# Where an expert's tokens sit in its half tile: consecutive rows, or rows 0, 8, 16, ... in turn

## The chip, the cores and the metric

One Trainium2 chip, one of its NeuronCores. The metric is the time of one execution on the device, in microseconds; the median of three executions of the kernel before is 883.63 us (880.76 to 884.49).

## What is computed

A float32 decoder trunk of two layers over 512 tokens of width 1024. Each layer is a mixer (gated spatial mixing and sparse attention in layer 0, a causal pooling in layer 1) and then a mixture of experts. Only the experts matter here:

```python
lg = xn @ w_rg + b_rg;  g_sel = argmax(lg)            # one of 4 groups
le_sel = (xn @ w_re + b_re)[group g_sel]              # 8 experts of the group
top_v, top_i = top_k(le_sel, 2)                       # the two best
h = silu(xn @ w_gate[e]) * (xn @ w_up[e])             # 1024 -> 256, each chosen expert
y += weight * (h @ w_down[e])                         # 256 -> 1024
```

There are 32 experts a layer, each with 3 MB of weights, and each token goes to two of them: 1024 token slots a layer. The slots that each expert gets come out of the router. Computed with the reference on its own inputs they are, two experts (a pair) at a time from pair 0 to pair 15:

```
layer 0: 29,39  17,25  41,30  51,34  24,39  45,29  35,27  54,47  28,21  16,43  19,43  29,29  30,17  27,25  32,42  31,26
layer 1: 18,22  25,16  19,16  21,15  21,26  49,39  37,36  49,45  42,51  23,49  32,41  46,30  19,21  21,40  42,41  43,29
```

## The kernel before, in words

**The pair loop.** The experts of a layer are worked off in 16 pairs. A pair has a tile of 128 rows: 64 for its first expert, 64 for its second. `slot0` (line 634) gives each expert its base, and a token's slot is that base plus the token's rank within the expert, so the 39 tokens of an expert have ranks 0 to 38. What would overflow 64 goes to extra pairs; with the counts above there is none, and the code for them (lines 678 to 692) runs no iteration.

**The tables.** `route` (DVE, lines 1361 to 1473) turns the routing into two tables of row numbers with one-hot matrices. Line 1438 is where the row of the tile is fixed: `OA[p, a, n]` is 1 where `col128[n]` equals the token's slot number within the pair (`pm`). Before, `col128[n] = n` (line 630). TensorE multiplies `OA` by the pair one-hots (line 1884), and the result, indexed by row n and pair, becomes `gather_at` (line 1446) and `scatter_at` (line 1444). A row without a token gets the number 4096 for the scatter and 3584 for the gather, which the bounds check leaves out. The last pair is not scattered: its rows are added by a matmul with `pair_mix`, which is made of the same `OA` (lines 1466 to 1473). So everything that uses the row order takes it from `OA`.

**The transfers of a pair.** POOL issues a gather of a pair's token rows from `norm_dram` into `xg` (line 653, 128 row numbers, 4 KB a row, one SBUF partition a row) and, after the pair is computed, a scatter of its result rows from `ys` into `out_dram` (line 659). That makes 16 gathers and 15 scatters a layer. The gather of pair i + 2 is issued once TensorE has transposed pair i. SP issues the weights in the order of use into three buffers (lines 535 to 568): four transfers of 1 MB for gate and up, two of 1 MB for down; the last pair's down comes in halves. A weight transfer writes the same bytes to each of the 128 partitions. SP waits for TensorE to have finished pair i - 3 before it loads pair i.

**Engines.** TensorE transposes the gathered rows (line 1892), does gate and up (line 1898, 32 recorded matmuls a pair), transposes the hidden rows (line 1905) and does down (line 1912, 16). It waits for a pair's weights by semaphore. After the last pair come the sums over the two experts of a token (lines 1110, 1114, 2000), for which SP reads `out_dram` back (line 572).

**Data movement.** All transfers run on the core's 16 DMA engines. A transfer counts as landed when every engine that had a part of it is through with that part.

Of the kernel before, what the change touches and what calls it, by code (L numbers as in the profile page):

```python
# [24 lines left out]
P = 128  # L25
# [11 lines left out]
TILE = 64  # L37
# [8 lines left out]
def build(nc, t):  # L46
    ctx = ExitStack()
    with ctx:
        def sb(name, cols, dt=F32, parts=P):
            return ctx.enter_context(nc.sbuf_tensor(name, [parts, cols], dt))  # L50
# [18 lines left out]
        col128 = sb("col128", P)  # L69
# [333 lines left out]
        def _(sp):  # L403
# [15 lines left out]
            def load_win(ch):  # L419
                _, c0, n = CH[ch]  # L420
                dst = win[ch % 2][:, 0:KD * n].rearrange("p (k n) -> p k n", k=KD)
                src = t["w_in"][0].rearrange("(p k) n -> p k n", k=KD)[:, :, c0:c0 + n]
                sp.dma_start(dst, src).then_inc(s_w[ch], 16)
# [168 lines left out]
        def _(pool):  # L592
            g = nc.gpsimd
            count = [0]

            def link(ins):

                count[0] += 1
                ins.then_inc(s_gp, 1)
                pool.wait_ge(s_gp, count[0])  # L600
# [26 lines left out]
            select(c3[0], NEG, -31, [[P, NB], [-16, 32]], 1)  # L627
            select(c3[1], 0.0, -31, [[P, NB], [-16, 32]], 1)
            io = dict(allow_small_or_imprecise_dtypes=True)
            link(g.iota(col128[:, :], [[1, P]], base=0, channel_multiplier=0, **io))  # L630
            link(g.iota(col32[:, :], [[1, 32]], base=0, channel_multiplier=0, **io))
            link(g.iota(tok_lo[:, :], [[0, 1]], base=0, channel_multiplier=1, **io))
            link(g.iota(tok_hi[:, :], [[1, 2 * NB]], base=-int(EMPTY) // P, channel_multiplier=0, **io))
# [1445 lines left out]
```

## Time and profile before

| | |
|---|---|
| median of 3 executions | 883.63 us |
| the profiled execution | 885.34 us, its span 883.6 us |
| TensorE busy | 790.1 us, mean granted clock 0.967 |
| DVE, ACT, POOL busy | 249.8, 244.6, 99.6 us |
| mean DMA rate over the span | 292 GB/s |
| packets of the POOL queue (gathers, scatters) | 16.27 MB in 8928 packets |
| packets of the SP queue | 241.16 MB in 67056 packets |

The profile has two expert stages. In layer 0 the loads of pair 3 are issued at 335 us and the last pair's gate and up finish at 556 us; in layer 1 these are 635 and 861 us. In both the DMA engines move some 420 GB/s, and outside of them much less. "Granted clock" is the share of full speed at which TensorE was allowed to run. "issue" in a chain is time in which an engine waited for nothing that the profile records. The profiled execution was 1.7 us slower than the median.

### The profile page before, as it was taken

What the parts mean: (1) busy time and instruction counts of PE and PEld (TensorE: products, weight loads), DVE (VectorE), ACT (ScalarE), POOL (GpSimd) and SP (SyncE); (2) the same over time, 40 slices, a digit from 0 to 9 for tenths busy, and PEclk for the clock granted to TensorE, in tenths of its full rate; (3) what the DMA queues carried; (4) which work ended last, traced back from release to release, by engine and by line L of the source; (5) the groups of instructions that cost most, each with busy time, mean ns of one, the idle gap of its engine ahead of it and who ended that gap; (6) DMA issues with size and microseconds to landing.
All of it is one profiled execution on the core that took longest, in us unless ns stands there. A gap on an engine that the chain in (4) does not pass through costs nothing.

```text
span 883.6 us, 10297 instructions
## 1 busy us (share of the span) xinstructions
PE 790.1 (89%) x3966; PEld 376.2 (43%) x3973; DVE 249.8 (28%) x565; ACT 244.6 (28%) x587; POOL 99.6 (11%) x167
## 2 busy tenths in 40 slices
PE   7999999999999989999787987898999987797975
PEld 6544544454555633333332332496433332232321
DVE  1012428566452351111011111545411110111106
ACT  4321436644344401211111111454121221111101
POOL 2000000000003510111001010040111111101000
PEclk9999999999999999999998999999999998898998
DMA  7996130300003987999999999997399999999975
GB/s 257 237 330 256 55 96 1 96 1 1 1 1 99 342 352 297 418 420 419 421 422 419 418 409 376 387 421 318 136 400 420 419 420 421 422 419 416 413 302 228
DMA packets 76032, 258.09 MB, mean 292 GB/s; under 512 B 28113, under 2 KB 29649, under 8 KB 56016
## 3 DMA queue, kind: packets, MB, share of 16 engines
q1 hardware_dynamic: 67056, 241.16, 69.8%
q0 software_dynamic: 8928, 16.27, 4.9%
q8 instruction: 32, 0.52, 0.2%
q14 instruction: 16, 0.13, 0.0%
HBM read 247.44 MB, written 26.21 MB: 310 GB/s over the span
## 4 chain that ended last, share of the span: by engine, by line
PE 75%; DMA 8%; DVE 6%; issue 4%; ACT 3%; SPq 3%; DVEq 0%; POOLq 0%; ACTq 0%
PE ps L1898 23%; PE ps L1624 11%; PE ps L1912 11%; PE ps L1776 6%; PE ps L1892 4%; DMA w_pair<-in_w_exp_up_dram 3%; PE ps L1689 3%; DMA rest<-in_w_exp_down_dram 2%; PE ps L1832 2%; SPq L443 2%; PE ps L1701 2%; PE ps L1844 2%; PE ps L2027 2%; PE ps L1606 2%; PE ps L1589 2%
## 5 line engine op out<-in xcount | busy, mean ns | idle before, releaser
L1898 PE MATMUL ps<-w_pair,tmp 128*64 128x512 f32 x704 | 170.9, 640 | 34.8 <-issue 21.3
L1898 PEld LDWEIGHTS ps<-w_pair,tmp 128*64 128x64 f32 x704 | 55.8, 147 | 136.1 <-issue 122.5
L1624 PE MATMUL ps<-w_pair,norm 128*128 128x512 f32 (+1 forms) x256 | 100.5, 553 | 1.4 <-ACT norm L803 1.4
L1088 DVE TENSOR_TENSOR tmp<-tmp,ps 128x256 f32<-128x256 f32 (+1 forms) x34 | 13.8, 407 | 294.8 <-ACT tmp L973 294.7
L973 ACT ACTIVATE tmp<-ps 128x256 f32<-128x256 f32 x32 | 12.3, 383 | 271.4 <-PE ps L1898 271.4
L1898 PE MATMUL ps<-norm,tmp 128*64 128x512 f32 x320 | 74.8, 621 | 12.2 <-issue 9.2
L1912 PE MATMUL ps<-w_pair,tmp 128*64 128x512 f32 x352 | 80.4, 598 | 3.1 <-ACT tmp L976 2.0
L1624 PEld LDWEIGHTS ps<-w_pair,norm 128*128 128x128 f32 x256 | 49.4, 195 | 49.3 <-issue 44.6
L659 POOL DMA_INDIRECT expert_rows<-tmp x30 | 30.1, 1003 | 327.0 <-DVE tmp L1491 327.0
L1776 PE MATMUL ps<-w_pair,norm 128*128 128x512 f32 x128 | 58.0, 593 | 0.0
L968 ACT ACTIVATE tmp<-ps,gains 128x128 f32<-128x128 f32 x128 | 36.5, 368 | 62.3 <-PE ps L1892 62.3
L1898 PEld LDWEIGHTS ps<-norm,tmp 128*64 128x64 f32 x320 | 23.3, 143 | 56.3 <-issue 51.3
L1491 DVE COPY tmp<-ps 128x512 f32<-128x512 f32 x30 | 20.7, 691 | 93.3 <-PE ps L1912 93.3
L653 POOL DMA_INDIRECT tmp<-norm_rows,tmp x32 | 32.7, 1022 | 119.9 <-DVEq L1448 54.3
L1892 PEld LDWEIGHTS ps<-ident,tmp 128*128 128x128 f32 x256 | 31.9, 195 | 32.6 <-issue 30.4
L1892 PE MATMUL ps<-ident,tmp 128*128 128x128 f32 x256 | 38.2, 294 | 7.5 <-issue 6.7
L1912 PEld LDWEIGHTS ps<-w_pair,tmp 128*64 128x64 f32 x352 | 23.7, 136 | 43.4 <-issue 38.7
L984 ACT ACTIVATE tmp<-ps 128x512 f32<-128x512 f32 x30 | 17.9, 597 | 82.7 <-PE ps L1912 82.7
L932 ACT ACTIVATE rest<-ps 128x768 f32<-128x768 f32 (+3 forms) x32 | 21.6, 676 | 63.8 <-PE ps L1832 63.8
L1589 PE MATMUL ps<-masks 128*128 128x512 bf16 x163 | 38.7, 392 | 0.4
L1912 PE MATMUL ps<-rest,tmp 128*64 128x512 f32 x160 | 36.5, 597 | 2.5 <-DMA rest<-in_w_exp_down_dram 2.5
L900 ACT ACTIVATE rest<-ps,mix_small 128x384 f32<-128x384 f32 (+3 forms) x64 | 32.2, 511 | 3.4 <-DVE mix_small L1294 3.1
(254 smaller groups left out, 831.6 us busy)
## 6 DMA issues: line engine op xcount, KB each, us to landing
w_pair<-in_w_exp_gate_dram SPq DMA_DIRECT2D x44, 1024.0 KB, 17.8
w_pair<-in_w_exp_up_dram SPq DMA_DIRECT2D x44, 1024.0 KB, 23.1
w_pair<-in_w_exp_down_dram SPq DMA_DIRECT2D x40, 1024.0 KB, 25.3
rest<-in_w_exp_down_dram SPq DMA_DIRECT2D x20, 1024.0 KB, 23.7
norm<-in_w_exp_gate_dram SPq DMA_DIRECT2D x20, 1024.0 KB, 22.9
norm<-in_w_exp_up_dram SPq DMA_DIRECT2D x20, 1024.0 KB, 25.0
w_pair<-in_w_in_dram SPq DMA_DIRECT2D x4, 2048.0 KB, 13.5
norm<-expert_rows SPq DMA_DIRECT2D x16, 512.0 KB, 8.3
```

The source lines that it names most:

```text
L653: return pool.indirect_dma_start(out=buf, out_offset=None, in_=norm_dram, in_offset=bass.IndirectOffsetOnAxis(ap=index, axis=0), bounds_ch ...
L659: return pool.indirect_dma_start(out=out_dram, out_offset=bass.IndirectOffsetOnAxis(ap=index, axis=0), in_=buf, in_offset=None, bounds_che ...
L900: ins = a.activation(prob[:, n % 2, h, 0:width], bank(2 * (n % 2) + h)[:, 0:width], ACT.Exp, bias=nmax[:, 2 * n + h:2 * n + h + 1], accum_ ...
L932: a.activation(pT[:, n % 2, 0:nb], ps[2][:, :, :].rearrange("p c n -> p (c n)")[:, 0:256 * nb] .rearrange("p (a h t) -> p a h t", h=2, t=P ...
L968: ins = a.activation(xgT[:, k, :], bank(0)[:, k * P:(k + 1) * P], ACT.Copy, scale=gain_v[:, n, k:k + 1])
L1589: mm(o, identb, masks[:, 0:512], start=True, stop=True)
L1624: ins = mm(bank(4 + i % 4)[:, 0:n], xT[:, k, b * P:(b + 1) * P], w[:, k, :], start=(k == 0), stop=(k == KD - 1))
L1689: ins = mm(bank(7), xT[:, k, b * P:(b + 1) * P], w[:, k, :], start=(k == 0), stop=(k == KD - 1))
L1776: ins = mm(out_bank(b, half), xT[:, k, b * P:(b + 1) * P], wout[half][:, k, :], start=(j == 0), stop=(j == KD - 1))
L1892: ins = te.transpose(bank(k // 4)[:, (k % 4) * P:(k % 4 + 1) * P], xv[:, k, :], ident[:, :])
L1898: ins = mm(bank(2)[64 * a:64 * a + 64, :], xgT[:, k, 64 * a:64 * a + 64], gu[w][:, a, :, k * FE:(k + 1) * FE], start=(k == 0), stop=(k == ...
L1912: ins = mm(bank(4 + half)[64 * a:64 * a + 64, :], hidT[:, jj, 64 * a:64 * a + 64], dn[w][:, a, c0:c0 + 512], start=(jj == 0), stop=(jj == 1))
```

## The change

One line of the kernel's set-up on POOL. The 128 entries of `col128` were 0, 1, 2, ... 127. Now entry n = 64 t + 8 i + j (t below 2, i and j below 8) is 64 t + i + 8 j.

```diff
             io = dict(allow_small_or_imprecise_dtypes=True)
-            link(g.iota(col128[:, :], [[1, P]], base=0, channel_multiplier=0, **io))
+
+            link(g.iota(col128[:, :], [[TILE, 2], [1, 8], [8, 8]], base=0, channel_multiplier=0, **io))
             link(g.iota(col32[:, :], [[1, 32]], base=0, channel_multiplier=0, **io))
```

The token with rank r of an expert now sits in row 8 (r mod 8) + r div 8 of the expert's 64 rows: ranks 0 to 7 in rows 0, 8, ... 56, ranks 8 to 15 in rows 1, 9, ... 57, and so on. An expert with 32 tokens filled rows 0 to 31 and now fills rows 0 to 3, 8 to 11, 16 to 19 and so on up to 56 to 59. The tables, the gathers, the scatters and `pair_mix` follow, since all come from `OA`; each row goes back to the token it came from. Nothing else is edited, and no instruction is added.

## Rows read from the trace of the kernel before

**Rows 1.** Page: engine shares, DMA per slice, and the chain that ended last

```profile
PE 790.1 (89%) x3966; PEld 376.2 (43%) x3973; DVE 249.8 (28%) x565; ACT 244.6 (28%) x587; POOL 99.6 (11%) x167
...
DMA  7996130300003987999999999997399999999975
...
PE 75%; DMA 8%; DVE 6%; issue 4%; ACT 3%; SPq 3%; DVEq 0%; POOLq 0%; ACTq 0%
```

**Rows 2.** Stretches: length; busy of PE, PEld, DVE, ACT, POOL; clock, DMA share, GB/s

```profile
335.15:552.85 217.70, 190.37 (x875) 73.19 (x871) 27.06 (x45) 36.55 (x106) 28.25 (x28) 0.96 1.00 407
635.16:855.44 220.28, 191.69 (x875) 73.70 (x871) 27.06 (x45) 36.51 (x106) 28.22 (x28) 0.95 0.99 404
353.00:541.00 188.00, 166.09 (x759) 63.95 (x758) 23.82 (x40) 32.30 (x94) 25.28 (x25) 0.95 1.02 418
```

**Rows 3.** Chain in layer 0: start, us, what (one pair, then pairs kept waiting)

```profile
377.72 7.02 PE ps L1898 x32
384.74 1.09 PE ps L1892 x8
385.83 3.58 PE ps L1912 x16
389.41 0.44 PE ps L1905 x2
...
414.10 1.50 issue
...
427.81 4.58 issue
...
520.13 21.29 DMA rest<-in_w_exp_down_dram
```

**Rows 4.** TensorE's last gate and up halves: start, us, and idle time before

```profile
552.85 3.65 PE L1898 MATMUL ps<-w_pair,tmp 128*64 128x512 f32 x16 [2.49 <-DMA w_pair<-in_w_exp_up_dram]
...
855.44 5.35 PE L1898 MATMUL ps<-w_pair,tmp 128*64 128x512 f32 x16 [2.05 <-DMA w_pair<-in_w_exp_up_dram]
```

**Rows 5.** SP's issue that opens the loads of pair 3, layers 0 and 1

```profile
335.15 0.38 SPq L436 DMA_DIRECT2D w_pair<-in_w_exp_gate_dram  x1
...
635.16 0.38 SPq L436 DMA_DIRECT2D w_pair<-in_w_exp_gate_dram  x1
```

**Rows 6.** Stretch with layer 1's first gather alone on the DMA engines

```profile
625.50:626.60 1.10, 1.10 (x6) 0.49 (x5) 1.07 (x6) 0.00 (x0) 0.76 (x1) 1.00 0.55 138
```

**Rows 7.** Stretches at the end of both expert stages

```profile
541.00:545.00 4.00, 3.49 (x16) 1.26 (x16) 0.00 (x0) 0.00 (x1) 1.00 (x1) 1.00 0.94 374
545.00:549.00 4.00, 2.46 (x14) 1.05 (x14) 0.69 (x1) 0.60 (x1) 0.98 (x1) 1.00 0.94 363
549.00:553.00 4.00, 1.51 (x10) 0.37 (x8) 0.00 (x0) 0.00 (x0) 0.00 (x0) 1.00 0.67 264
...
843.00:847.00 4.00, 2.90 (x14) 1.26 (x16) 0.00 (x0) 0.01 (x1) 1.00 (x1) 1.00 0.75 302
847.00:851.00 4.00, 2.02 (x10) 0.57 (x8) 0.69 (x1) 0.60 (x1) 0.97 (x1) 1.00 0.85 312
851.00:855.00 4.00, 2.39 (x12) 0.69 (x8) 0.00 (x0) 0.00 (x0) 0.00 (x0) 1.00 0.65 256
```

**Rows 8.** Gathers and scatters: their lines' landing times (layer 0's fourth issue below)

```profile
L653 POOL DMA_INDIRECT tmp<-norm_rows,tmp x32: 987/1017/1226, 318.6 to 815.9; - x32
...
DMA to landing us min/median/max: 3.4/10.2/12.2
...
367.62 1.02 POOL L653 DMA_INDIRECT tmp<-norm_rows,tmp  x1 [0.30 <-issue]
```

**Rows 9.** The edited instruction

```profile
L630 POOL IOTA col<- x1: 238/238/238, 6.7 to 6.7; 128x128 f32 x1
```

**Rows 10.** The same two TensorE halves as stretches, for the clock

```profile
552.85:556.50 3.65, 3.65 (x16) 1.05 (x16) 0.00 (x0) 0.00 (x0) 0.00 (x0) 1.00 0.76 275
855.40:860.80 5.40, 5.35 (x16) 1.46 (x16) 0.00 (x0) 0.00 (x0) 0.00 (x0) 0.68 0.82 287
```

## The prediction

> **What bounds the kernel now.** I read the page first. TensorE is busy 89% of the span, which looks like the bound; but the line of DMA shares stands at nines through both expert stages [rows 1]. Of two nearly full resources one has to be shown to wait for the other. One pair costs TensorE 7.02 + 1.09 + 3.58 + 0.44 = 12.1 us when nothing is missing [rows 3]. The pair's six weight transfers of 1 MB put 393,216 bytes on each of 16 DMA engines. At 418 GB/s [rows 2] an engine moves 26.1 GB/s, so that is 15.1 us before any token row. The DMA engines are the slower of the two. The chain agrees: TensorE runs pair after pair on weights loaded ahead until 414 us, then pauses of 1.5 and 4.6 us appear, and near the end the chain runs through a transfer of 21.29 us [rows 3]. Both stages end with TensorE waiting for the last pair's up weights [rows 4]. What the change does to compute is therefore nothing; what it does to the DMA engines counts.
>
 I weigh three splits, with the table of slots given ahead:
>
> - *fours*: each engine has two blocks of four consecutive rows of one half tile, 32 rows apart (rows 0 to 3 and 32 to 35 on one engine, 4 to 7 and 36 to 39 on the next);
> - *eights*: each engine has eight consecutive rows;
> - *sixteenths*: row n goes to engine n mod 16.
>
> Three readings decide between them. First, layer 1's first gather (18 + 22 rows) has the engines to itself; fours give it 5 + 6 = 11 engines, eights 3 + 3 = 6, sixteenths all 16. The stretch that holds it shows a share of 0.55, that is 8.8 engines on average with the ramp inside, at 138 GB/s over 1.10 us = 37 of the 40 rows [rows 6]. Six engines can't reach that share. Second, a stage runs from SP's issue of pair 3 [rows 5] to the up weights of pair 15. Until then an engine carries 76 transfers of 65,536 bytes, 76 x 2.51 = 190.8 us, plus its rows of 13 gathers and 14 scatters. The fullest engine's rows in layers 0 and 1 are: fours 152 and 168, eights 216 and 216, sixteenths 131 and 139; the mean is 108 and 111. With 0.157 us a row that makes 214.7 and 217.2 us for fours, 224.7 twice for eights, 211.4 and 212.6 for sixteenths. Measured are 217.70 and 220.28 [rows 2]. Eights are too long to be possible; fours are 3.0 and 3.1 short (the ramp after 335 us), and they alone give the 2.6 us between the layers (16 rows x 0.157 = 2.5). Third, the rate falls toward the end while weights are still awaited: 374, 363, 264 GB/s, and earlier and deeper in layer 1 [rows 7]. Some engines are dry while others have work, which is what 152 rows on one and 50 on another would leave.
>
> So the kernel is bound by its fullest DMA engines, not by the mean of the 16, and the split is in fours.
>
> [...]
>
> **The change, part by part.**
>
> *The instruction.* One iota with another pattern, 0.24 us near 6.7 us [rows 9], long before the first use at layer 0's tables. Cost nothing. If the new pattern took three times as long, the set-up that TensorE does not need yet would still hide it.
>
> *The rows on the fullest engine.* Before, an expert with c slots put 4 rows on its half's first engine, and up to 4 more when c is above 32: 4 + min(4, max(0, c - 32)). Now ranks below 32 fill the first four rows of every block of eight, and these belong to the even engines of the half; ranks above 31 go to the odd ones. The first engine has the ranks divisible by 4 below 32: min(c, 32) / 4 rounded up. For an expert of 21 that is 6 instead of 4, for one of 29 it is 8 instead of 4, for one of 43 it is 8 either way. Summed over 13 gathers and 14 scatters for the second experts (their half is the fuller one): layer 0 from 152 to 96 + 104 = 200, layer 1 from 168 to 192. The emptiest engine goes from 50 to 19, and from 56 to 32. The change doesn't spread the rows, it gathers them on half the engines.
>
> *Price.* 48 rows x 0.157 = 7.5 us in layer 0 and 24 x 0.157 = 3.8 us in layer 1. All of it lies on the path: TensorE's last pair waits for the fullest engine in both stages [rows 4], and behind it the work is a fixed tail. SP issues a weight transfer to all engines at once and two to three pairs ahead, so the fullest engines are never out of work, and the others being dry costs nothing more. Bounds: 0, if the order in the queues hides it; 11.3 us, since the fullest engine's extra rows can't delay it by more than their own time. I take the upper end, because the stages before measured what their fullest engine demands, to within 3.1 us.
>
> *Gathers and scatters landing later.* A gather that had 4 rows on its deepest engine now has up to 8, and in between the engine serves weights. With one 4 KB row and one 8 KB weight packet in turn (0.157 + 0.314 us), 4 rows more are 1.9 us. Landing took 10.2 us in the median; the gather issued at 367.62 is needed at 384.74, so 5 to 7 us of slack remain [rows 3, 8]. I take 0; the bounds are 0 and 1.9 us a layer (the gathers around pair 11 and the last scatter, which have less slack).
>
> [...]
>
> *Sum.* The profiled execution of 885.34 us + 11.3 = 896.6. It stood 1.7 us above the median of 883.63, so against the median I predict **895**.
>
> **The rivals.**
>
> 1. *Eights* (ends faster). If a gather's eight consecutive rows share an engine, the change is a gain: the fullest engine falls from 216 to 123 and 125 rows, 93 x 0.157 + 91 x 0.157 = 28.9 us less, 855 us. It decides as soon as the engine of a row follows from row div 8. Against it: the share in [rows 6], and stages 7.0 and 4.4 us shorter than it demands [rows 2]. [...]
> 2. *Sixteenths.* The change puts 8 neighbouring residues to full: 131 to 216 and 139 to 216 rows, 162 x 0.157 = 25.4 us more, 909 us. Against it: 40 rows on 16 engines would be over in half the time seen [rows 6], and the layers would differ by 1.3 us, not 2.6.
> 3. *No change.* The rows are not tied to engines by their place, or weights wait elsewhere: 883.6. Against it: the falling rates in [rows 7].
> 4. *Fours with additions.* Both late gathers and a slow clock in layer 0: 11.3 + 3.8 + 1.7 = 16.8, 900 us. Part of the main case's upper end.
>
> **How the numbers follow.** The main case with its additions has 0.82, eights 0.04, sixteenths 0.05, no change 0.09. About 0.5% (4.4 us) is what a measurement can tell from no change here. The main case reaches from 889, where half of the extra rows is hidden, to 901; that range holds about 8 in 10 and leaves out most of the other three. Faster by over 0.5%: 0.04. Within 0.5%: no change and a main case almost wholly hidden, 0.10. Slower: 0.86.
>
> **What the profile of the changed kernel would show.** Right: the stretch from SP's issue of pair 3 to the last up weights grows by about 7 us in layer 0 and 4 in layer 1; the difference between the layers turns round, to layer 0 as long as or longer than layer 1; the DMA share in the last 20 us of both stages drops well under 1, toward 0.6, while TensorE waits; layer 1's first gather shows 8 engines instead of 11, 5 or 6 rows deep; TensorE's busy time stays near 790 us. Wrong: a stage shorter than 217 us (eights), a saturated rate to the end with equal lengths (no change), or a growth over 12 us in one layer (sixteenths).

## The result, and the profile after

| | before | changed |
|---|---|---|
| median | 883.31 us (4 executions) | 902.74 us (4 executions, 901.59 to 903.16) |
| ratio | | 1.0214, 95% interval 1.0188 to 1.024 |
| profiled execution | 885.34 us, span 883.6 us | 902.58 us, span 900.8 us |

The changed kernel is slower by 19.4 us, and by 17.2 us between the two profiled executions. The forecast was 895 us, 11.4 us slower: the right way, but too little, and the result lies above the range. In 28 later executions of the kernel before, in three groups, the medians of the groups were 883.67 to 884.82 us.

The page of the changed kernel: engine shares, DMA per slice, and the chain that ended last. They answer to [rows 1].

```profile
PE 795.8 (88%) x3966; PEld 377.5 (42%) x3973; DVE 250.0 (28%) x565; ACT 244.9 (27%) x587; POOL 99.8 (11%) x167
...
DMA  7996130300005969999999988996499999999985
...
PE 66%; DMA 18%; DVE 6%; SPq 4%; ACT 3%; issue 3%; DVEq 1%; POOLq 0%
```

TensorE's work is what it was, within 6 us of busy time. What changed is that the chain now goes through DMA for 18% of the span instead of 8%, and that the row of nines has eights and a six in it.

Three stretches of the changed kernel (length; busy time of PE, PEld, DVE, ACT, POOL; clock, DMA share, GB/s): each stage from SP's issue of pair 3 to the last up weights, and layer 1's first gather. They answer to [rows 2, 6].

```profile
336.17:562.87 226.70, 192.05 (x874) 73.13 (x870) 27.08 (x45) 36.61 (x106) 28.25 (x28) 0.95 0.97 392
646.66:872.68 226.02, 192.16 (x874) 73.96 (x870) 27.08 (x45) 36.59 (x106) 28.21 (x28) 0.95 0.98 393
...
637.00:638.10 1.10, 1.10 (x6) 0.49 (x5) 1.07 (x6) 0.00 (x0) 0.76 (x1) 1.00 0.43 75
```

Layer 0's stage grew from 217.70 to 226.70 us, layer 1's from 220.28 to 226.02 us; layer 0 is now the longer one. The same 40 rows of the first gather now keep 0.43 x 16 = 6.9 engines busy instead of 8.8, at 75 GB/s instead of 138. The semaphore records of the two traces are sharper. The gather's semaphore is raised 16 times: before, 5 times up to 626.04 us and 11 times from 626.47 us on, and in the changed kernel 8 times up to 637.63 us and 8 times from 638.46 us on. Read as one raise by each engine, the early ones by those that have no filled row, 11 and 8 are the engine counts that fours give.

The end of layer 0's stage in the changed kernel, in stretches (against [rows 7]), and an earlier stretch of it:

```profile
521.00:525.00 4.00, 4.00 (x11) 1.08 (x9) 0.00 (x0) 0.00 (x0) 0.00 (x0) 0.50 0.51 211
...
551.00:555.00 4.00, 3.09 (x16) 0.92 (x12) 0.69 (x1) 0.60 (x1) 0.65 (x1) 1.00 0.88 333
555.00:559.00 4.00, 3.36 (x16) 1.26 (x16) 0.00 (x0) 0.00 (x0) 0.98 (x1) 1.00 0.78 289
559.00:562.80 3.80, 0.29 (x2) 0.00 (x0) 0.00 (x0) 0.00 (x0) 0.00 (x0) 1.00 0.52 206
```

Share 0.51 and 0.52: about eight of the sixteen engines are at work. The first of these stretches lies 185 us into the stage, and there the packet records show eight packets under way for 87% of it and nine for 13%. The second is the end of the stage, where TensorE does almost nothing but wait. That the other eight have nothing left in their queues is read from this half share and the layout of the rows; no view shows the queues.

TensorE's last gate and up halves in both layers (start, us, idle time before it), against [rows 4]:

```profile
562.87 5.35 PE L1899 MATMUL ps<-w_pair,tmp 128*64 128x512 f32 x16 [3.58 <-DMA w_pair<-in_w_exp_up_dram]
...
872.68 5.35 PE L1899 MATMUL ps<-w_pair,tmp 128*64 128x512 f32 x16 [3.13 <-DMA w_pair<-in_w_exp_up_dram]
```

**Where 17.2 us went**, between the two profiled executions: 9.0 us in layer 0's stage, 5.7 us in layer 1's, 1.5 us between the stages (the half pair that took 3.65 us in layer 0 takes 5.35 us now, as it had in layer 1 all along), 1.0 us before the first stage, 0 behind the second. The piece before the first stage is no effect: over all kernels of this study, pair 3 of layer 0 is issued between 332.2 and 336.8 us, without order.

### The profile page after: what moved, and what is told of

Same layout as the page of the kernel before. It is cut to its first block, busy times and chain, and to the rows that moved or that the text cites. A ratio compares the mean times of both kernels' runs of the same rounds, so it can differ in the third digit from the quotient of the medians.

```text
span 900.8 us, 10297 instructions
## 1 busy us (share of the span) xinstructions
PE 795.8 (88%) x3966; PEld 377.5 (42%) x3973; DVE 250.0 (28%) x565; ACT 244.9 (27%) x587; POOL 99.8 (11%) x167
## 3 DMA queue, kind: packets, MB, share of 16 engines
q0 software_dynamic: 8928, 16.27, 4.8%
## 4 chain that ended last, share of the span: by engine, by line
PE 66%; DMA 18%; DVE 6%; SPq 4%; ACT 3%; issue 3%; DVEq 1%; POOLq 0%
PE ps L1899 20%; DMA w_pair<-in_w_exp_up_dram 12%; PE ps L1625 11%; PE ps L1913 8%; PE ps L1777 6%; DMA norm<-in_w_exp_up_dram 3%; PE ps L1690 3%; PE ps L1833 2%; PE ps L1893 2%; PE ps L1702 2%; PE ps L1845 2%; PE ps L1607 2%; PE ps L2028 2%; PE ps L1590 1%; SPq L443 1%
## 5 line engine op out<-in xcount | busy, mean ns | idle before, releaser
L1899 PE MATMUL ps<-w_pair,tmp 128*64 128x512 f32 x704 | 174.6, 652 | 46.6 <-DMA w_pair<-in_w_exp_up_dram 24.9
L1913 PE MATMUL ps<-w_pair,tmp 128*64 128x512 f32 x352 | 80.4, 598 | 4.8 <-issue 2.8
```

The costliest lines, as they stand in the source:

```text
L1899: ins = mm(bank(2)[64 * a:64 * a + 64, :], xgT[:, k, 64 * a:64 * a + 64], gu[w][:, a, :, k * FE:(k + 1) * FE], start=(k == 0), stop=(k == ...
L1913: ins = mm(bank(4 + half)[64 * a:64 * a + 64, :], hidT[:, jj, 64 * a:64 * a + 64], dn[w][:, a, c0:c0 + 512], start=(jj == 0), stop=(jj == 1))
```

## The experiments

All are named by what they do. "The fullest engine's rows" are those of 13 gathers and 14 scatters, counted in fours as in the prediction. Stage lengths are those between the same two events as above.

### Four orders of the rows

e1_round_robin deals ranks out over the blocks of four, e2_stacked fills one engine after the other, e3_odd_blocks is the changed order four rows further:

```diff
-            link(g.iota(col128[:, :], [[TILE, 2], [1, 8], [8, 8]], ...))
+            link(g.iota(col128[:, :], [[TILE, 2], [1, 16], [16, 4]], ...))   # e1_round_robin
+            for ha in range(2):                                              # e2_stacked
+                for hb in range(2):
+                    link(g.iota(col128[:, 64 * ha + 32 * hb:64 * ha + 32 * hb + 32], [[8, 8], [1, 4]],
+                                base=64 * ha + 4 * hb, ...))
+            cv = col128[:, :].rearrange("p (t i h j) -> p t h i j", t=2, i=8, h=2)   # e3_odd_blocks
+            for ha in range(2):
+                for hb in range(2):
+                    link(g.iota(cv[:, ha, hb], [[1, 8], [8, 4]], base=64 * ha + 32 * (1 - hb), ...))
```

> The rank r of an expert now sits in row 4 (r mod 16) + r div 16 of its half tile, so neighbouring ranks go to different blocks of four rows. If a DMA engine owns two such blocks 32 rows apart and the fullest engine sets the stage, its rows in 13 gathers and 14 scatters fall from 152 (before) and 200 (changed) to 123 in layer 0, and from 168 and 192 to 125 in layer 1. The four stages measured so far (217.7, 220.3 us before, 226.7, 226.0 us changed) lie on a line of 0.20 us a row, so theory A expects stages of about 212 us in both layers and a total near 870 us, 13 to 14 us under before. Rival B, that the changed kernel is slow because half of the engines run dry, expects the time of before or a few us less, since before had few dry engines until the last 12 us. Rival C, a row costs 0.157 us and the rest of the 19 us came from TensorE's clock and late gathers: 872 to 876 us.

> Ranks 0 to 7 fill both blocks of one engine, 8 to 15 both of the next, and so on: the fullest engine gets 216 rows in each layer, the emptiest none, and only two or three engines of eight are full. Theory A (fullest engine, 0.20 us a row): 64 and 48 rows over before are 12.8 and 9.6 us, with 1.7 us for a slow clock in layer 0 about 907 us, stages near 230 and 229 us. Rival B (what costs is the number of engines that are full or dry): here fewer engines are full than in the changed kernel, so 890 to 900 us. Rival C (0.157 us a row): 17.6 us over before plus what the changed kernel lost besides, 901 to 904 us.

> The changed order moved by four rows: ranks below 32 fill rows 4 to 7, 12 to 15 and so on, that is the odd blocks of four, ranks above 31 the even ones. The rows per engine are those of the changed kernel with neighbours swapped. Theory A: the changed kernel's time within 2 us, 901 to 904 us. If some property of the even engines or of their partitions was what cost the additional time beyond 0.157 us a row, this comes out at 895 to 898 us.

| | rows, layers 0, 1 | stages, us | median | ratio to before |
|---|---|---|---|---|
| e1_round_robin | 123, 125 | 215.03, 215.61 | 876.23 | 0.9907 (0.9878 to 0.9936) |
| before | 152, 168 | 217.70, 220.28 | 883.91 | |
| changed | 200, 192 | 226.70, 226.02 | 902.74 | 1.0214 |
| e3_odd_blocks | 200, 192 | 226.61, 228.23 | 902.62 | 1.0213 (1.0181 to 1.0246) |
| e2_stacked | 216, 216 | 231.84, 232.92 | 911.00 | 1.0312 (1.0279 to 1.0345) |

Both stages of e1_round_robin and of e2_stacked in the view of stretches:

```profile
332.96:547.99 215.03, 190.49 (x874) 73.19 (x870) 27.06 (x45) 36.62 (x106) 28.25 (x28) 0.96 1.01 411
631.14:846.75 215.61, 190.02 (x874) 72.54 (x870) 27.06 (x45) 36.57 (x106) 28.20 (x28) 0.96 1.01 412
```

```profile
333.69:565.53 231.84, 193.54 (x875) 73.06 (x871) 27.07 (x45) 36.61 (x106) 28.26 (x28) 0.94 0.95 385
649.68:882.60 232.92, 195.56 (x875) 74.52 (x871) 27.07 (x45) 36.57 (x106) 28.20 (x28) 0.93 0.96 384
```

Both stages of e3_odd_blocks:

```profile
336.13:562.74 226.61, 194.08 (x875) 74.99 (x871) 27.08 (x45) 36.75 (x106) 28.27 (x28) 0.95 0.97 392
646.52:874.75 228.23, 191.80 (x874) 74.35 (x870) 27.09 (x45) 36.71 (x106) 28.21 (x28) 0.95 0.97 391
```

The order of the fullest engine's rows is the order of the stages, in both layers, and no other edit is made. Which engines are full, even or odd, changes nothing in layer 0. In layer 1 the odd blocks took 2.2 us longer with the same rows, which is open; these stages come from one profile each, and two profiles that should agree, of the kernel before and of e8_before_warm below, differ by 1.2 us there (220.28 and 221.50) and by 0.1 us in layer 0. So layer 0's stages are the sharper measure. The equal medians of the two kernels hide this: in layer 1 e3_odd_blocks ran its last half pair in 3.65 us, not 5.35. But theory A's straight line of 0.20 us a row fell: from 152 to 123 rows only 2.7 us are gained where 5.8 were expected, and from 200 to 216 it is 5.1 us where 3.2 were. Rival C's 0.157 throughout misses both ends as well.

### One full engine

The first engine of each half tile gets the changed kernel's share; everything else is dealt out to the other seven. `col128` is written by single memsets on POOL, in the time before POOL waits for the attention:

```diff
+            for half_tile in (0, 64):
+                for q in range(56):
+                    rank = q + q // 3 + 1 if q < 24 else q + 8
+                    k = q // 7
+                    ins = place(half_tile + 4 * (1 + q % 7) + k % 4 + 32 * (k // 4), half_tile + rank)
+                for k in range(8):
+                    ins = place(half_tile + k % 4 + 32 * (k // 4), half_tile + 4 * k)
```

> Only the first engine of each half tile is filled as in the changed kernel (it gets the ranks divisible by 4 below 32, in all 200 rows of layer 0 and 192 of layer 1 over 13 gathers and 14 scatters); the other ranks are dealt in turn to the other seven engines, which get 85 to 115 rows. The table col128 is written by 128 small memsets on POOL while it would wait for the attention. Theory A (the fullest engine alone sets the stage): stages of 226 to 227 us in both layers, a total of 901 to 903 us, as the changed kernel, although 14 of 16 engines are lighter than the fullest ones before. Theory D (the additional 1.5 to 2 us a layer come from eight engines being nearly equally full, so that the latest of eight decides, or from the other eight running dry): stages of 224 to 225 us, 897 to 899 us. Theory E (the mean or the number of full engines sets the stage): at or under the time of before, 876 to 884 us.

Measured: 900.31 us, ratio 1.0184 (1.0159 to 1.021), stages of 226.60 and 224.55 us. Both stages, and the last stretch before layer 0's last up weights:

```profile
332.56:559.16 226.60, 193.11 (x874) 73.39 (x870) 27.06 (x45) 36.55 (x106) 28.25 (x28) 0.95 0.97 394
644.00:868.55 224.55, 191.84 (x875) 74.10 (x871) 27.06 (x45) 36.52 (x106) 28.21 (x28) 0.94 0.98 398
...
555.70:559.10 3.40, 0.00 (x0) 0.00 (x0) 0.00 (x0) 0.00 (x0) 0.00 (x0) 1.00 0.18 67
```

This is the plainest line of the study. For 3.4 us every compute engine stands still, about three of sixteen DMA engines work on average (0.18 x 16 = 2.9) and 67 GB/s flow: a kernel whose mean DMA load is the same as e1_round_robin's loses 24 us to one engine of each half tile. Layer 0 is as long as in the changed kernel to 0.1 us, so there the seven other full engines have no part in it, and neither have the dry ones. Theory E is out: the time is 16 us above its range. Theory D fell in layer 0 only: layer 1's 224.55 us is 1.5 us under the changed kernel's stage, where D had put it and not theory A, and the total lies between the two ranges. After what e3_odd_blocks showed of layer 1, 1.5 us there decide nothing, so a small part of the other full engines in layer 1 is not excluded.

### What a row costs

e6_no_rows, e11_before_gathers and e12_after_gathers take the data away and leave all instructions:

```diff
-                        bounds_check=SEQ - 1, oob_is_err=False)
+                        bounds_check=0, oob_is_err=False)        # gathers: e6_no_rows
-                        bounds_check=2 * SEQ - 1, oob_is_err=False)
+                        bounds_check=0, oob_is_err=False)        # scatters: e6_no_rows, e11, e12
```

> The kernel before with the bounds of all gathers and scatters set to 0, so that only row 0 is ever moved and the experts compute on stale rows; all instructions and semaphores stay. Leaves out the transfer of the token rows. The stages then show what the weights alone demand: at 2.51 us a transfer of 1 MB, 76 of them and 1 to 2 us of ramp are 192 to 193 us. Theory A with one price per row: from 215.0 and 215.6 us with 123 and 125 rows on the fullest engine that would be 0.18 us a row. If the stages come out at 196 us or more, a row costs 0.157 us or less in a balanced kernel, and what the changed kernel paid beyond that is something else.

> The kernel before with the scatters' bound set to 0: result rows aren't written, gathers are whole (leaves out the scatters' data; layer 1 then routes other tokens, so only layer 0 is read). The fullest engine has 74 gathered rows, the fullest with all transfers 152. Layer 0's stage with no rows at all was 198.30 us, with all 217.70 us. If a row costs the same in a gather and in a scatter: 198.3 + 74 x 0.128 = 207.8 us.

> The changed kernel with the scatters' bound set to 0; 96 gathered rows on the fullest engine in layer 0, 22 more than e11_before_gathers. The whole change added 9.0 us to layer 0's stage for 48 rows, 0.19 us a row. If gathers and scatters share this alike, the stage is 22 x 0.19 = 4.1 us longer than that of e11_before_gathers. If the price beyond 0.157 us comes with the scatters (rows written to HBM), 3.5 us or less; if with the gathers, 5 us or more.

Layer 0's stage of e6_no_rows, e11_before_gathers and e12_after_gathers, in this order:

```profile
333.78:532.08 198.30, 185.56 (x874) 70.17 (x870) 27.05 (x45) 36.55 (x106) 28.25 (x28) 0.98 1.01 408
```

```profile
335.34:542.71 207.37, 189.87 (x875) 71.75 (x871) 27.07 (x45) 36.62 (x106) 28.33 (x28) 0.96 1.01 408
```

```profile
334.04:544.97 210.93, 188.79 (x874) 72.68 (x871) 27.06 (x45) 36.55 (x106) 28.26 (x28) 0.97 1.00 402
```

Without the rows' data the stage takes 198.3 us, not 192 to 193. This is a little more than the weights alone: a row that is left out still makes a packet of 4 bytes. The page of e6_no_rows counts 32074 packets under 512 B, that of the kernel before 28113. From 198.3 to e1_round_robin's 215.03 us the 123 rows cost 0.136 us each, under 0.157, so by the expectation what the changed kernel paid beyond is something else than one price for all rows. The 74 gathered rows of e11_before_gathers cost 0.12 us each (207.37 us, 207.8 expected).

With 22 more gathered rows on the fullest engine the stage is 3.56 us longer: 0.162 us a row, near the price that I had taken. The change as a whole added 9.00 us for 48 rows, so its 26 additional scattered rows have the other 5.44 us: 0.21 us a row. That does not show that a scattered row is dearer. The gathers were compared at 74 and 96 rows on the engine and the whole at 152 and 200, and the next experiments show that the price depends on the number of rows already there. The surplus can be in the scatters, in having both, or in the number of rows.

### The same engine at 152, 200 and 216 rows

The variants of e5_one_full differ in which block is filled and with which ranks: multiples of 4 (200 rows in layer 0), 0 to 3 and 32 to 35 (152, as before), 0 to 7 (216). BLOCK and `first` stand for the values of each variant.

```diff
-                    ins = place(half_tile + 4 * (1 + q % 7) + k % 4 + 32 * (k // 4), half_tile + rank)
+                    ins = place(half_tile + 4 * ((BLOCK + 1 + q % 7) % 8) + k % 4 + 32 * (k // 4), half_tile + rank)
-                    ins = place(half_tile + k % 4 + 32 * (k // 4), half_tile + 4 * k)
+                    ins = place(half_tile + 4 * BLOCK + k % 4 + 32 * (k // 4), half_tile + first[k])
```

> As e5_one_full, but the engine that gets the ranks divisible by 4 is the last of each half tile (rows 28 to 31 and 60 to 63) instead of the first; the rows per engine are the same, shifted by seven places. e5_one_full had stages of 226.60 and 224.55 us and 900.3 us. Without any rows both stages still took 198.3 us, 2 to 3 us more than the packets' own durations add up to, and the gate and up packets of the last pair end on one or two engines about 2 us after the rest. Theory F (one engine of each half, the last, is slower with the weights alone, which is why the balanced kernels take 215 us and why before is cheap for its fullest engine): stages of 229 to 231 us, 904 to 908 us. Theory A with equal engines: 226.6 us in layer 0, 899 to 903 us.

> The control for e9_block7_full: the fourth engine of each half tile (rows 12 to 15 and 44 to 47) is the full one. Both theories, A and F, expect e5_one_full's stage of 226.6 us in layer 0 and 899 to 903 us; a spread of more than 1 us against e5_one_full would say that engines differ in some other way.

> As e5_one_full (first engine of each half tile full, the others dealt out), but that engine gets ranks 0 to 7, which is 216 rows in layer 0 instead of 200 (and 216 instead of 192 in layer 1). e5_one_full's stage in layer 0 was 226.60 us. A constant marginal price of 0.16 us a row (as the gathers showed) gives 229.2 us, 0.19 (the whole change) 229.6 us, 0.33 (changed kernel to e2_stacked) 231.8 us. At 231 us or more the bend is in the single engine's own rows; at 229 to 230 us e2_stacked's remainder came from its neighbours.

> The first engine gets ranks 0 to 3 and 32 to 35, that is exactly the rows that it has in the kernel before (142 and 152 in layer 0, 156 and 168 in layer 1), all other ranks are dealt out over the other seven (91 to 115 rows). If the fullest engine alone decides, layer 0's stage is before's 217.6 us. If before's other filled engines (145, 136, 133 rows) had a part, it is shorter, 215 to 216 us.

> The same with the last engine (rows 28 to 31 and 60 to 63). e9_block7_full with 200 rows there had a stage of 224.51 us in layer 0, 2.1 us less than e5_one_full. If the last engine is simply faster by a constant 2.1 us, the stage is 215.5 us unless another engine then decides; its own price per row is (224.5 - this stage) / 48, expected 0.19 us.

> The last engine with 216 rows. At 0.19 us a row from e9_block7_full's 224.51 us: 227.6 us in layer 0; at 0.33 us a row 229.8 us.

| layer 0's stage, us | 152 rows | 200 rows | 216 rows |
|---|---|---|---|
| block 0 | 217.49 | 226.60 | 231.97 |
| block 3 | | 227.74 | |
| block 7 | 216.99 | 224.51 | 228.76 |

| layer 1's stage, us | 168 rows | 192 rows | 216 rows |
|---|---|---|---|
| block 0 | 219.68 | 224.55 | 230.05 |
| block 3 | | 225.88 | |
| block 7 | 220.26 | 223.63 | 228.32 |

In time: e9_block7_full 897.04 us (ratio 1.0144, 1.0119 to 1.017), e10_block3_full 901.88 us (1.0197, 1.0168 to 1.0226); of the others one execution each was taken, 907.80, 884.30, 885.11 and 903.92 us. Stages of e14_block0_152, e13_block0_216 and e9_block7_full, and for the latter two a stretch at the end:

```profile
334.12:551.61 217.49, 190.52 (x874) 73.61 (x871) 27.07 (x45) 36.62 (x106) 28.33 (x28) 0.96 1.00 409
```

```profile
332.19:564.16 231.97, 194.72 (x875) 74.44 (x871) 27.05 (x45) 36.55 (x106) 28.26 (x28) 0.94 0.95 385
560.50:564.10 3.60, 0.00 (x0) 0.00 (x0) 0.00 (x0) 0.00 (x0) 0.00 (x0) 0.98 0.21 81
```

```profile
335.28:559.79 224.51, 191.97 (x874) 74.36 (x870) 27.07 (x45) 36.62 (x106) 28.32 (x28) 0.94 0.98 397
556.30:559.70 3.40, 0.02 (x1) 0.00 (x0) 0.00 (x0) 0.00 (x0) 0.00 (x0) 0.85 0.20 80
```

In layer 0 e14_block0_152 is the kernel before to 0.2 us (0.6 us in layer 1), though its second to eighth engines are lighter: before, too, the fullest engine alone decided. Theory F fell, and the other way round: with 192 rows and more the last block's engines are the cheapest in both layers, by 0.9 to 3.2 us against block 0. With 152 and 168 rows there is no such order (0.5 us less in layer 0, 0.6 us more in layer 1). From 152 to 216 rows layer 0 pays 14.5 / 64 = 0.23 us a row on block 0 and 11.8 / 64 = 0.18 us on block 7; from 168 to 216 layer 1 pays 0.22 and 0.17. The price rises with the rows, and this doesn't need the neighbours to be full: in layer 0 on block 0 0.19 us a row up to 200 and 0.34 beyond, on block 7 0.16 and 0.27. Layer 1 bends less: 0.20 and 0.23, 0.14 and 0.20. The figures at 152 and 216 rows rest on one execution each, and the steepest on 16 rows; from 200 to 216 the fullest engine of the other half tile rises too, from 191 to 216 rows.

### The clock at the end of a stage

```diff
                     for h in range(2):
+                        if i == MAIN - 1 and h == 1:
+                            keep_warm(10, bank(7))      # 8 in e7_round_robin_warm and e8_before_warm
                         pe_.wait_ge(s_gul[h][w], 32 * slot_fill(l, i))
```

> The changed kernel, with ten 128x512 bf16 matmuls on TensorE before it waits for the second half of the last pair's gate and up weights, in both layers. In the changed kernel that half took 5.35 us in both layers after pauses of 3.6 and 3.1 us, and before 3.65 us in layer 0 and 5.35 us in layer 1. If the pause is what lets the clock fall, the half takes 3.65 us in both layers and the total falls by 3.4 us, to about 899.5 us. If the clock follows something longer ago, the half stays at 5.35 us and the time at 902.7 us.

> The kernel before with the same eight matmuls. Layer 1's half falls from 5.35 to 3.65 us, layer 0's stays at 3.65 us: 1.7 us under before, near 882 us. It separates the clock's part of the changed kernel: if before gains 1.7 us and the changed kernel gained about 3.4 us of its 5.5 us by the clock, the rest of that gain was scatter between runs.

> The dealt-out order of e1_round_robin with eight 128x512 bf16 matmuls before the wait for the second half of the last pair's weights. In e1_round_robin that half took 3.65 us in layer 0 and 5.35 us in layer 1, so 1.7 us are to be had: about 874.5 us against 876.2 us. If the matmuls delay anything, at or above 876 us.

The last half of e4_warm_last in both layers, with the matmuls that fill the wait (timeline of TensorE):

```profile
557.10 2.33 PE L1590 MATMUL ps<-masks 128*128 128x512 bf16 x10
560.75 3.65 PE L1899 MATMUL ps<-w_pair,tmp 128*64 128x512 f32 x16 [1.31 <-DMA w_pair<-in_w_exp_up_dram]
...
865.87 2.33 PE L1590 MATMUL ps<-masks 128*128 128x512 bf16 x10
869.19 3.65 PE L1899 MATMUL ps<-w_pair,tmp 128*64 128x512 f32 x16 [1.00 <-DMA w_pair<-in_w_exp_up_dram]
```

With the wait filled, the half pair takes 3.65 us in both layers at a granted clock of 1.00, 2 x 1.7 = 3.4 us less than in the changed kernel. The pause is not the whole cause, though. In e2_stacked's layer 1 the half pair took 3.65 us after a pause of 3.10 us that nothing filled, in e15_block7_152's layer 0 5.35 us after one of 2.22 us, and in e5_one_full's layer 1 it took 6.58 us at a granted clock of 0.55, so the clock's share in a stage's end is not bounded by 1.7 us either. The medians of e4_warm_last and the changed kernel are 897.22 and 902.74 us, 5.5 us apart; of the 5.2 us between their profiles 1.8 us lie before the first stage, where nothing was edited. e8_before_warm measured 883.58 us, ratio 0.9984 (0.9967 to 1.0), so what it gains isn't told from nothing with certainty. e7_round_robin_warm measured **874.02 us**, ratio 0.9875 (0.9851 to 0.9898), faster than both kernels by this edit of two places.

## Why the prediction missed

**What was right.** The readings that the count of rows rests on hold in the runs. A transfer landed with its slowest engine: in e5_one_full the semaphore of layer 0's last up weights is raised 12 times up to 545.15 us, then at 552.54, 555.25, 555.62 and 559.12 us, and TensorE's last half starts at 559.16 us. The weights loaded all 16 engines alike: over layer 0's stage of e6_no_rows, 198.30 us almost without rows, the DMA share is 1.01, and 16 or more packets are under way for 99% of it. Right were the bound (DMA engines, not TensorE), the split in fours, the rule that the fullest engine sets both stages (in layer 0 to 0.2 us, while layer 1's profiles differ by 1 to 2 us at equal rows), the 48 and 24 additional rows, that nothing else in the kernel moves, and the signs: layer 0 grew more than layer 1 and overtook it, the share falls to 0.5 at the end. e5_one_full and e14_block0_152 show the rule by itself. The rivals eights, sixteenths and no change are out: eights wanted 29 us less, sixteenths 12 to 13 us more in each layer, against 9.0 and 5.7 us.

**The step that failed is the price of a row.** I took 0.157 us, the engine's time for 4096 bytes at the stage's mean rate, "since the fullest engine's extra rows can't delay it by more than their own time". They did: 9.0 / 48 = 0.19 us in layer 0 and 5.7 / 24 = 0.24 us in layer 1, together 14.7 us instead of 11.3. e5_one_full, with only one full engine in each half tile, confirms layer 0's 0.19 us; in layer 1 it gives 4.3 / 24 = 0.18. What looked like a confirmation was not one. The stages before came out 3.0 and 3.1 us over weights plus rows, which I read as a ramp. Without any row the stage is 198.3 us, 7.5 us over my 190.8 for the weights, and 152 rows add 19.4 us to it, 0.128 each. A base too low and a price too high for the rows up to there came near the right sum at 152 and 168 rows, and that was luck; the price at the margin, which alone counts for a change, is neither. The bound from above was not one for the same reason: a row's own transfer time is not all that it costs the engine.

**Two readings were off without harm to the difference.** An empty row does not move nothing but makes a packet of 4 bytes: of the POOL queue's 8928 packets before, 3967 have 4096 bytes (159 ns each in the median), together 16.25 of its 16.27 MB, and 4961 have 4 bytes (9 ns each): 3969 empty rows, and 16 more for each of the 62 transfers. And a stage has 15 scatters, not 14. The last one of layer 0, that of pair 14, is issued while the last weights are still under way:

```profile
546.66 0.98 POOL L659 DMA_INDIRECT expert_rows<-tmp  x1 [4.04 <-DVE tmp L1491]
```

Its 8 rows on the fullest engine are the same before and after, so the 48 and 24 additional rows stay. But they belong to what I called a ramp: in e5_one_full's packet records eight packets of 4 KB from POOL's queue alternate one for one with the last weight packets of the engine that finishes last, at 155 ns from one start to the next, which is 1.2 us. So the packets of the rows themselves took no longer than the price assumed, and the surplus must lie elsewhere.

**The clock was taken at the wrong end.** For a slow last half in layer 0 the forecast's range has 0 to 1.7 us, the 5.35 less 3.65 us of the two halves in [rows 4], and I took 0, expecting that it could come with longer pauses. That a longer pause alone brings it, no run shows: the half took 3.65 us after 3.10 us of idling (e2_stacked, layer 1) and 5.35 us after 2.22 us (e15_block7_152, layer 0). It came, 1.5 us between the stages, and it is gone in e4_warm_last, where the wait is filled. Layer 1 had already paid it before. Late gathers, the other addition, did not come: in layer 0's stage TensorE waited for a gather once, for 0.8 us before and 0.7 us in the changed kernel, and a gather's median time to landing was 10.2 and 10.6 us.

**The reference.** I subtracted 1.7 us because the profiled execution of before stood above its median. The changed kernel's did not (902.58 against 902.74 us), and pair 3's issue wanders by 4.6 us between kernels that are equal up to there. Of the 7.7 us that were missing, 3.4 are the price, 1.5 the clock, and about 3 this. The range, too, was built on the first price and reached only 6 us up; with the prices measured here, 0.16 to 0.24 us for 72 rows and the clock, it would have been 12 to 19 us, and the measured 19.4 us still lies at its end.

**What stays open** is why the price rises with the rows already on an engine (in layer 0 0.09 us a row from 123 to 152, 0.19 to 200, 0.32 to 216 by e2_stacked and 0.34 by the single block; in layer 1 0.11 from 125 to 168, 0.24 to 192, 0.29 to 216 by the four orders). A part of the low start has an explanation that was not tried by itself: up to some row count another engine than the fullest one finishes last, since the engines weren't equal (224.51 to 227.74 us at 200 rows). The steep end, on both blocks tried, has none here. Whether scattered rows are dearer than gathered ones is not shown: it was read from layer 0 alone, in one profile each, and at different numbers of rows.

## What to carry to other kernels

When all DMA engines look busy, ask which rows share an engine: here a stage bound by transfers, with few rows in many slots, was as long as its fullest engine made it (in layer 0 215.03 us with 123 rows on it, 226.70 us with 200), and dealing the rows out by blocks of four (here 4 x (r mod 16) + r div 16 in a half tile of 64) gave 7.7 us for one line, where "every eighth row" cost 19. Take the price of one more row from two kernels that differ in rows, not from bytes over bandwidth (0.19 us in layer 0, not 0.157), and test the base by itself before trusting that the sum fits (198.3 us without rows, not 190.8). In e5_one_full a stretch in which every compute engine was idle, 3.4 us at a DMA share of 0.18, showed the full engines' excess directly.

## What was not expected of the hardware

- Engines did not cost the same. With the last block of each half tile full the stages were the shortest of the three blocks tried (7 against 0 and 3): 224.5 us against 226.6 and 227.7 us at 200 rows in layer 0, and 223.6 against 224.6 and 225.9 us at 192 rows in layer 1, in one profile each. At 152 and 168 rows no difference was clear.
- One more token row of 4 KB on the fullest engine cost more than its bytes once the engine had about 150 of them: 0.19 us from 152 to 200 rows in layer 0, against 0.157 us by the stage's rate and 155 ns between the packets themselves (e5_one_full). From 123 to 152 rows it cost 0.09 us.
- The clock of the last half's 16 matmuls did not follow from the pause before them alone: after 2.49 us of idling it ran at a granted clock of 1.00 (before, layer 0), after 2.05 us in layer 1 it took 5.35 us at 0.68, and after 3.10 us it ran at 1.00 again (e2_stacked, layer 1). With ten small matmuls (2.33 us) ahead of the last 1.31 and 1.00 us of the wait it ran at 1.00 both times (e4_warm_last).
